# The first two products of down's first groups as split products, their tokens' low parts made in the group ahead

## The chip, the cores and the metric

One core of one Trainium2 chip. The metric is the device time in microseconds (us) of one execution of the whole program. Engines: PE is TensorE, PEld its weight loads, DVE is VectorE, ACT is ScalarE, POOL is GpSimd, SP is the engine that issues most DMAs.

## What is computed

One layer of a hybrid decoder in fp32: an input projection, a short convolution and an mLSTM, an output projection, and then a SwiGLU feed-forward block, which is all that matters here:

```python
hn = _rmsnorm(x, n2g)
x = x + (jax.nn.silu(hn @ wg) * (hn @ wu)) @ wd
```

There are 512 + 64 tokens, `D_MODEL` is 2048 and `D_FF` 5632, which is `FT` = 44 tiles of 128.

## The kernel before, in words

**Split products.** fp32 accuracy is had from the rounded type fp32r. Each operand is split into a high part (a copy rounded to fp32r, made by ACT) and a low part (the operand less its high part, made by DVE). A product is then three matmuls for each tile of 128 rows: high by high, high by low and low by high (L836, L838, L840 in `product`). With `GK` = 8 tiles that is 24 matmuls of 128x128 weights by 288 tokens.

**Groups of seven products.** The feed-forward block is done two by two in blocks with Strassen's scheme in Winograd's form: each group is seven products (p = 0 to 6) instead of eight. Groups 0 to 43 are gate and up; the 16 *down groups* d = 0 to 15 (`FT + d`) are the down product's first 32 tiles of hidden values, in two halves (`NCH` = 2) of `PPC` = 8 groups. The rest of down follows in an ordinary way. Products 0, 2, 4 and 6 of a group accumulate into one PSUM bank, `bank_a`. After product 4 DVE must take a sum out of it (`upper_up`, L2149, in gate and up; `add_block(d, 1)`, L2265, in down), and signals that by `c22_ok`; only then may product 6 go on in the same bank:

```python
pe.wait_ge(c22_ok, g + 1)
product(m, u, 6, bank_a, False)
```

**Order on each engine.** Each engine has one stream of instructions, written out by hand, and waits at semaphores. ACT makes a product's high weights into a ring of three slots (`product_hi`, L1259), when the product three back has been used. DVE makes the low weights (`product_low`, L2095; it counts `g_lo`), and sums of weight blocks (`weight_sum`, L2077 to L2090; n = 1 is for the group to come). DVE runs ahead of PE by some products, so the last sums of group g stand in DVE's code for group g + 1: `down_group(0)` begins on DVE with `upper_up` of group 43, and `down_group(d)` with `add_block(d - 1, 1)`.

**The first group of each half.** The operands on the token side (seven tensors `opraw[j]`, j = 0 to 6) change at d = 0 and d = 8. SP loads `opraw[j]` (L478) when product j of the group ahead has been used. ACT makes the high parts (`hidden_hi`, L1335, two halves of 128x1152) and DVE the low ones (`hidden_low`, L2244, two halves). The low part `oplo[j]` is written over `opraw[j]`, in the same memory. Down groups 0 and 8 use the raw operands: `whole_product` (L851) is 8 plain fp32 matmuls on a whole copy of the weights (`whole_copy`, L1268); on DVE `whole_ready` does only semaphore work. `hidden_low(c, j)` waits until product j of that group has read the raw tokens. ACT makes `hidden_hi` of j = 0 and 1 in the group ahead already (L1324 to L1328 and L1386 to L1392). On DVE `hidden_low` of j = 0 to 3 stands in down group 0 or 8 (L2298 to L2316), of j = 4 to 6 in the group behind it.

Of the kernel before, what the change touches and what calls it, by code (L numbers as in the profile page):

```python
# [60 lines left out]
def hybrid_trunk_step(nc, x_prompt, x_sample, state_conv, state_C, state_n, state_m, norm1_g, w_in,  # L61
# [14 lines left out]
    FT = FF // P  # L76
# [23 lines left out]
    X_PIECES = ((0, 2), (2, 2), (4, 4), (8, 4), (12, 4))  # L100
    SMALLS = 10
    SQ_ACT = 4
    X_LAST = {k0 + n - 1: b for b, (k0, n) in enumerate(X_PIECES)}
    assert sum(n for _, n in X_PIECES) == KT
    QS = float(DK) ** -0.5
    GK = KT // 2
    GU = 6
# [5 lines left out]
    NCH, PPC = FS // KT, KT // 2  # L113
# [7 lines left out]
    with ExitStack() as ctx:  # L121
# [461 lines left out]
        def _(pe):  # L583
# [326 lines left out]
            def down_group(d):  # L910
                g = FT + d
                m, u = g // GU, g % GU
                bank_a, bank_b, bank_c = BANK_A[u % 3], 1, 4
                for p, bank, start, ready, n in ((0, bank_a, True, c21_ok, g - 2), (1, bank_c, True, c12_ok, g),
                                                 (2, bank_a, False, p1c_ok, g + 1), (3, bank_b, True, c11_ok, g),
                                                 (4, bank_a, False, u2c_ok, g + 1), (5, bank_c, False, p5c_ok, g + 1),
                                                 (6, bank_a, False, c22_ok, g + 1)):
                    pe.wait_ge(ready, n)
                    if d % PPC == 0:
                        whole_product(m, u, p, bank, start, d // PPC)  # L920
                    else:
                        if d % PPC == 1:
                            pe.wait_ge(op_lo, 15 + 14 * (d // PPC) + 2 * p + 2)
                        product(m, u, p, bank, start)
                    if p == 3 and d > PPC:
                        turn_pair(d - 1)
# [76 lines left out]
        def _(act):  # L1003
# [354 lines left out]
            def down_group(d):  # L1358
                g = FT + d
                m, u = g // GU, g % GU  # L1360
                c, bank_a, bank_c = d // PPC, BANK_A[u % 3], 4
                starts = d % PPC == 0
                ends = d % PPC == PPC - 1 and c + 1 < NCH
                weights = whole_copy if starts else product_hi
                weights(m, u, 0)
                weights(m, u, 1)
                if d == 0:
                    gate_sigmoid(g)
                weights(m, u, 2)
                if starts:  # L1370
                    hidden_hi(c, 2)
                keep_copy(m, u, 0, p1c, bank_a, c11_ok, p1c_ok)
                weights(m, u, 3)
                if starts:
                    hidden_hi(c, 3)
                weights(m, u, 4)
                keep_copy(m, u, 1, p5c, bank_c, c22_ok, p5c_ok)
                if starts:
                    hidden_hi(c, 4)
                keep_copy(m, u, 2, u2c, bank_a, c12_ok, u2c_ok)  # L1380
                if d == 0:
                    h_store(m, u)
                weights(m, u, 5)
                if starts:
                    hidden_hi(c, 5)
                if ends:  # L1386
                    hidden_hi(c + 1, 0)
                weights(m, u, 6)
                if starts:
                    hidden_hi(c, 6)  # L1390
                if ends:
                    hidden_hi(c + 1, 1)  # L1392
                if 1 <= d <= PPC:
                    sum_store(d - 1)
                elif d > PPC:
                    turned_out(d - 1)
# [146 lines left out]
        def _(dve):  # L1543
# [548 lines left out]
            def product_low(m, u, p):  # L2092
                dve.wait_ge(g_hi, m * (7 * GU) + (7 * u + p + 1))
                slot = (7 * u + p) % 3
                tt(gw_ring[:, slot, 1], source(u, p), gw_ring[:, slot, 0].bitcast(F32), ALU.subtract).then_inc(g_lo, 1)  # L2095
# [90 lines left out]
                             (th4[:, 0, :], b21, th32[:, 1, :]))[n]  # L2186
                tt(out, a, b, ALU.subtract).then_inc(t_step, 1)

            def group(m, u, norm=None):

                g = m * GU + u
                v = (u - 1) % GU
                pair = u % 2 == 0 and (not isinstance(m, int) or g <= FS)

                def sums(n):
                    if pair:
                        pair_sum(m if u else m - 1, v, n)

                upper_up(g - 1, v)
                product_low(m, u, 0)  # L2200
                weight_sum(m, u, 2)
                lower_gate(g - 1)
                if norm:
                    norm[0]()
                else:
                    gate_scaled(g - 1)
                weight_sum(m, u, 3)
                product_low(m, u, 1)
                if norm:
                    norm[1]()  # L2210
                product_low(m, u, 2)
                if norm:
                    dve.wait_ge(r2_ok, 1)
                    gate_scaled(g - 1)
                weight_sum(m, u, 4)
                gate_product(g - 1)
                product_low(m, u, 3)
                gate_rstd(g - 1)
                product_low(m, u, 4)
                hidden(g - 1, v)  # L2220
                sums(0)
                product_low(m, u, 5)
                sums(1)
                upper_gate(g, u)
                sums(2)
                if u < GU - 1:
                    weight_sum(m, u + 1, 1)
                else:
                    weight_sum(m + 1, 0, 1)
                sums(3)  # L2230
                product_low(m, u, 6)

            def whole_ready(m, u, p):

# [3 lines left out]

            def hidden_low(c, j):

                dve.wait_ge(g_used, 7 * (FT + c * PPC) + j + 1)
                for n, (k0, k1) in enumerate(((0, 4), (4, GK))):
                    dve.wait_ge(op_hi, 15 + 14 * c + 2 * j + n + 1)
                    tt(oplo[j][:, k0:k1, :], opraw[j][:, k0:k1, :], ophi[j][:, k0:k1, :].bitcast(F32),  # L2244
                       ALU.subtract).then_inc(op_lo, 1)
# [21 lines left out]
            def down_group(d):  # L2267
# [4 lines left out]
                starts = d % PPC == 0  # L2272
                ends = d % PPC == PPC - 1 and c + 1 < NCH
                second = d % PPC == 1
                low = whole_ready if starts else product_low
                upper_up(g - 1, (u - 1) % GU) if d == 0 else add_block(d - 1, 1)
                low(m, u, 0)
                weight_sum(m, u, 2)
# [16 lines left out]
                gate_rstd(g - 1) if d == 0 else add_block(d - 1, 3)  # L2295
                if second:
                    hidden_low(c, 6)
                if starts:  # L2298
                    hidden_low(c, 0)
                low(m, u, 4)  # L2300
                if d == 0:
                    hidden(g - 1, (u - 1) % GU)
                if starts:
                    hidden_low(c, 1)
                low(m, u, 5)
                if starts:
                    hidden_low(c, 2)
# [7 lines left out]
                if starts:  # L2315
                    hidden_low(c, 3)  # L2316
                else:
                    low(m, u, 6)

            def norm_start():  # L2320
                dve.wait_ge(ss2_mm, 1)
# [22 lines left out]
                for w in range(GU):  # L2344
                    group(m, w)
            for g in range(FS // GU * GU, FT):
                group(g // GU, g % GU)
            for d in range(NCH * PPC):
                down_group(d)

# [147 lines left out]
```

## Time and profile before

| | |
|---|---|
| median of 3 runs | 2502.27 us (2502.08 to 2504.0) |
| profiled execution | 2503.21 us, span 2501.5 us |
| PE busy | 2460.6 us (98%) |
| DVE busy | 1771.9 us (71%) |
| ACT busy | 894.8 us (36%) |
| mean granted clock of TensorE | 0.996 |

Times in the trace are us from the start of the span. A row of a timeline is: start, duration, engine, line, operation, output <- inputs, shapes, number of instructions merged; in brackets the engine's idle time before it and what ended it. PE's matmuls overlap in the records, so their pace is read from starts. A granted clock of 1.00 is 2.4 GHz, of 0.50 the half level, 1.2 GHz.

### The profile page before, as it was taken

What the parts mean: (1) busy time and instruction counts of PE and PEld (TensorE: products, weight loads), DVE (VectorE), ACT (ScalarE), POOL (GpSimd) and SP (SyncE); (2) the same over time, 40 slices, a digit from 0 to 9 for tenths busy, and PEclk for the clock granted to TensorE, in tenths of its full rate; (3) what the DMA queues carried; (4) which work ended last, traced back from release to release, by engine and by line L of the source; (5) the groups of instructions that cost most, each with busy time, mean ns of one, the idle gap of its engine ahead of it and who ended that gap; (6) DMA issues with size and microseconds to landing.
All of it is one profiled execution on the core that took longest, in us unless ns stands there. A gap on an engine that the chain in (4) does not pass through costs nothing.

```text
span 2501.5 us, 44517 instructions
## 1 busy us (share of the span) xinstructions
PE 2460.6 (98%) x17602; PEld 2394.8 (96%) x17602; DVE 1771.9 (71%) x2487; ACT 894.8 (36%) x1236; POOL 37.2 (1%) x60
## 2 busy tenths in 40 slices
PE   8999999999999998999999999999999999999998
PEld 7999999999999997999999999999999999999886
DVE  7576575575687668887787777877777867766435
ACT  5212222222233335343333433434444533544313
POOL 0000000000000000000000000000000000000100
PEclk9999999999999999999999999999999999999999
DMA  5333233333335665343343433443333755744722
GB/s 124 99 117 102 76 117 101 90 104 94 89 113 155 190 194 188 112 127 113 107 126 110 120 116 110 127 118 116 106 108 108 253 150 152 271 132 141 272 82 76
DMA packets 458922, 325.54 MB, mean 130 GB/s; under 512 B 14130, under 2 KB 429006, under 8 KB 456368
## 3 DMA queue, kind: packets, MB, share of 16 engines
q1 hardware_dynamic: 403704, 250.29, 33.9%
q10 hardware_dynamic: 51448, 58.42, 7.6%
q0 software_dynamic: 3584, 14.16, 1.5%
q8 instruction: 140, 2.29, 0.4%
q14 instruction: 46, 0.38, 0.0%
HBM read 264.49 MB, written 58.34 MB: 129 GB/s over the span
## 4 chain that ended last, share of the span: by engine, by line
PE 94%; DVE 3%; DMA 1%; ACT 1%; issue 1%; SPq 0%; DVEq 0%; ACTq 0%
PE ps L603 21%; PE ps L836 17%; PE ps L840 17%; PE ps L838 17%; PE ps L606 11%; PE ps L611 3%; PE ps L851 2%; PE ps L947 2%; PE ps L949 2%; PE ps L951 2%; DVE gw_ring L2095 0%; PE ps L955 0%; DMA xtok<-in_x_sample_dram 0%; PE ps L956 0%; PE ps L863 0%
## 5 line engine op out<-in xcount | busy, mean ns | idle before, releaser
L836 PE MATMUL ps<-ophi,gw_ring 128*128 128x288 f32 x3248 | 963.9, 297 | 15.8 <-ACT p1c L1286 6.6
L838 PE MATMUL ps<-oplo,gw_ring 128*128 128x288 f32 x3248 | 959.6, 295 | 0.0
L840 PE MATMUL ps<-ophi,gw_ring 128*128 128x288 f32 x3248 | 957.9, 295 | 0.0
L836 PEld LDWEIGHTS ps<-ophi,gw_ring 128*128 128x128 f32 x3248 | 610.8, 188 | 18.3 <-ACT p1c L1286 7.0
L840 PEld LDWEIGHTS ps<-ophi,gw_ring 128*128 128x128 f32 x3248 | 613.3, 189 | 0.0
L838 PEld LDWEIGHTS ps<-oplo,gw_ring 128*128 128x128 f32 x3248 | 611.5, 188 | 0.2
L1012 ACT ACTIVATE whi<-wraw 128x512 fp32r<-128x512 f32 x256 | 160.6, 631 | 600.9 <-PE ps L606 449.4
L603 PE MATMUL ps<-xhi,whi 128*128 128x288 f32 x1536 | 333.7, 299 | 0.0
L606 PE MATMUL ps<-xhi,wlo 128*128 128x288 f32 x1536 | 329.5, 296 | 0.0
L603 PE MATMUL ps<-xlo,whi 128*128 128x288 f32 x1536 | 329.4, 296 | 0.0
L2095 DVE TENSOR_TENSOR gw_ring<-graw_a,gw_ring 128x1024 fp32r<-128x1024 f32 x195 | 238.7, 1224 | 116.8 <-ACT gw_ring L1259 116.2
L1259 ACT ACTIVATE gw_ring<-graw_a 128x1024 fp32r<-128x1024 f32 x195 | 206.4, 1059 | 271.3 <-PE ps L840 256.5
L1559 DVE TENSOR_TENSOR wlo<-wraw,whi 128x512 fp32r<-128x512 f32 x256 | 179.3, 700 | 139.6 <-ACT whi L1012 138.0
L603 PEld LDWEIGHTS ps<-xhi,whi 128*128 128x128 f32 x1536 | 248.0, 189 | 4.0 <-issue 3.0
L603 PEld LDWEIGHTS ps<-xlo,whi 128*128 128x128 f32 x1536 | 248.4, 189 | 0.0
L606 PEld LDWEIGHTS ps<-xhi,wlo 128*128 128x128 f32 x1536 | 248.1, 189 | 0.0
L2095 DVE TENSOR_TENSOR gw_ring<-wsum,gw_ring 128x1024 fp32r<-128x1024 f32 x116 | 141.7, 1222 | 83.4 <-ACT gw_ring L1259 83.4
L1554 DVE TENSOR_TENSOR wraw<-wraw,vecs 128x512 f32<-128x512 f32 x224 | 149.0, 683 | 45.0 <-DMA wraw<-in_w_in_dram 20.7
L1259 ACT ACTIVATE gw_ring<-wsum 128x1024 fp32r<-128x1024 f32 x116 | 122.6, 1057 | 116.1 <-PE ps L840 109.7
L2095 DVE TENSOR_TENSOR gw_ring<-graw_b,gw_ring 128x1024 fp32r<-128x1024 f32 x95 | 116.3, 1224 | 54.1 <-ACT gw_ring L1259 53.6
L1259 ACT ACTIVATE gw_ring<-graw_b 128x1024 fp32r<-128x1024 f32 x95 | 100.6, 1059 | 130.5 <-PE ps L840 128.4
L603 PE MATMUL ps<-mixhi,whi 128*128 128x288 f32 x512 | 109.9, 296 | 0.6 <-DVE wlo L1559 0.6
(336 smaller groups left out, 2661.6 us busy)
## 6 DMA issues: line engine op xcount, KB each, us to landing
wraw<-in_w_in_dram SPq DMA_DIRECT2D x96, 512.0 KB, 3.8
graw_a<-in_w_ffn_gate_dram SPq DMA_DIRECT2D x59, 512.0 KB, 3.7
graw_a<-in_w_ffn_up_dram SPq DMA_DIRECT2D x59, 512.0 KB, 4.9
graw_a<-in_w_ffn_down_dram SPq DMA_DIRECT2D x42, 512.0 KB, 5.7
wraw<-in_w_out_dram SPq DMA_DIRECT2D x32, 512.0 KB, 4.1
opraw<-hop SPq DMA_DIRECT2D x14, 1152.0 KB, 10.3
graw_b<-in_w_ffn_gate_dram SPq DMA_DIRECT2D x29, 512.0 KB, 3.7
graw_b<-in_w_ffn_up_dram SPq DMA_DIRECT2D x29, 512.0 KB, 4.6
```

The source lines that it names most:

```text
L603: pe.matmul(out[:, a, :], whi[:, q, s, :], moving[:, 2 * k + a, :], start=first and moving is hi, stop=False)
L606: mm = pe.matmul(out[:, a, :], wlo[:, q, s, :], hi[:, 2 * k + a, :], start=False, stop=last)
L611: one = lambda out, lhsT, rhs, start=True, stop=True: pe.matmul(out, lhsT, rhs, start=start, stop=stop)
L836: pe.matmul(out, gw_ring[:, slot, 0, k, :], ophi[p][:, k, :], start=start and k == 0, stop=False, skip_group_check=True)
L838: pe.matmul(out, gw_ring[:, slot, 0, k, :], oplo[p][:, k, :], start=False, stop=False, skip_group_check=True)
L840: mm = pe.matmul(out, gw_ring[:, slot, 1, k, :], ophi[p][:, k, :], start=False, stop=k == GK - 1, skip_group_check=True)
L851: mm = pe.matmul(ps[:, bank, 0:HT], gw_whole[:, slot, 0, k, :], opraw[p][:, k, :], start=start and k == 0, stop=k == GK - 1, skip_group_ch ...
L1012: act.activation(whi[:, q, 0:n, :], wraw[:, q // 2, s0:s0 + n, :], ACT.Copy).then_inc(hi_done, 1)
L1259: act.activation(gw_ring[:, (7 * u + p) % 3, 0], source(u, p), ACT.Copy).then_inc(g_hi, 1)
L1554: tt(w, w, g, ALU.mult).then_inc(gained, 1)
L1559: tt(wlo[:, q, 0:n, :], wraw[:, q // 2, s0:s0 + n, :], whi[:, q, 0:n, :].bitcast(F32), ALU.subtract).then_inc(lo_done, 1)
L2095: tt(gw_ring[:, slot, 1], source(u, p), gw_ring[:, slot, 0].bitcast(F32), ALU.subtract).then_inc(g_lo, 1)
```

## The change

Products 0 and 1 (`SPLIT_OPS` = 2) of down groups 0 and 8 become split products: PE runs `product` for them and waits for their tokens' low parts (`op_lo`), ACT makes `product_hi` and DVE `product_low` for their weights. `hidden_low` of j = 0 and 1 moves on DVE from down group 0 or 8 into the last group ahead of it: `hidden_low(c, 0)` ahead of that group's `product_low` 6 and `hidden_low(c, 1)` behind it, without the wait for `g_used`. (`ends` is assigned twice; that changes nothing.)

```diff
@@ -100,6 +100,7 @@
     X_PIECES = ((0, 2), (2, 2), (4, 4), (8, 4), (12, 4))
     SMALLS = 10
     SQ_ACT = 4
+    SPLIT_OPS = 2
     X_LAST = {k0 + n - 1: b for b, (k0, n) in enumerate(X_PIECES)}
     assert sum(n for _, n in X_PIECES) == KT
     QS = float(DK) ** -0.5
@@ -916,10 +917,10 @@
                                                  (4, bank_a, False, u2c_ok, g + 1), (5, bank_c, False, p5c_ok, g + 1),
                                                  (6, bank_a, False, c22_ok, g + 1)):
                     pe.wait_ge(ready, n)
-                    if d % PPC == 0:
+                    if d % PPC == 0 and p >= SPLIT_OPS:
                         whole_product(m, u, p, bank, start, d // PPC)
                     else:
-                        if d % PPC == 1:
+                        if d % PPC <= 1:
                             pe.wait_ge(op_lo, 15 + 14 * (d // PPC) + 2 * p + 2)
                         product(m, u, p, bank, start)
                     if p == 3 and d > PPC:
@@ -1361,7 +1362,7 @@
                 c, bank_a, bank_c = d // PPC, BANK_A[u % 3], 4
                 starts = d % PPC == 0
                 ends = d % PPC == PPC - 1 and c + 1 < NCH
-                weights = whole_copy if starts else product_hi
+                weights = lambda m, u, p: (whole_copy if starts and p >= SPLIT_OPS else product_hi)(m, u, p)
                 weights(m, u, 0)
                 weights(m, u, 1)
                 if d == 0:
@@ -2186,7 +2187,7 @@
                              (th4[:, 0, :], b21, th32[:, 1, :]))[n]
                 tt(out, a, b, ALU.subtract).then_inc(t_step, 1)
 
-            def group(m, u, norm=None):
+            def group(m, u, norm=None, last=False):
 
                 g = m * GU + u
                 v = (u - 1) % GU
@@ -2228,7 +2229,11 @@
                 else:
                     weight_sum(m + 1, 0, 1)
                 sums(3)
+                if last:
+                    hidden_low(0, 0)
                 product_low(m, u, 6)
+                if last:
+                    hidden_low(0, 1)
 
             def whole_ready(m, u, p):
 
@@ -2238,7 +2243,8 @@
 
             def hidden_low(c, j):
 
-                dve.wait_ge(g_used, 7 * (FT + c * PPC) + j + 1)
+                if j >= SPLIT_OPS:
+                    dve.wait_ge(g_used, 7 * (FT + c * PPC) + j + 1)
                 for n, (k0, k1) in enumerate(((0, 4), (4, GK))):
                     dve.wait_ge(op_hi, 15 + 14 * c + 2 * j + n + 1)
                     tt(oplo[j][:, k0:k1, :], opraw[j][:, k0:k1, :], ophi[j][:, k0:k1, :].bitcast(F32),
@@ -2272,7 +2278,8 @@
                 starts = d % PPC == 0
                 ends = d % PPC == PPC - 1 and c + 1 < NCH
                 second = d % PPC == 1
-                low = whole_ready if starts else product_low
+                ends = d % PPC == PPC - 1 and c + 1 < NCH
+                low = lambda m, u, p: (whole_ready if starts and p >= SPLIT_OPS else product_low)(m, u, p)
                 upper_up(g - 1, (u - 1) % GU) if d == 0 else add_block(d - 1, 1)
                 low(m, u, 0)
                 weight_sum(m, u, 2)
@@ -2295,13 +2302,9 @@
                 gate_rstd(g - 1) if d == 0 else add_block(d - 1, 3)
                 if second:
                     hidden_low(c, 6)
-                if starts:
-                    hidden_low(c, 0)
                 low(m, u, 4)
                 if d == 0:
                     hidden(g - 1, (u - 1) % GU)
-                if starts:
-                    hidden_low(c, 1)
                 low(m, u, 5)
                 if starts:
                     hidden_low(c, 2)
@@ -2315,7 +2318,11 @@
                 if starts:
                     hidden_low(c, 3)
                 else:
+                    if ends:
+                        hidden_low(c + 1, 0)
                     low(m, u, 6)
+                    if ends:
+                        hidden_low(c + 1, 1)
 
             def norm_start():
                 dve.wait_ge(ss2_mm, 1)
@@ -2344,7 +2351,7 @@
                 for w in range(GU):
                     group(m, w)
             for g in range(FS // GU * GU, FT):
-                group(g // GU, g % GU)
+                group(g // GU, g % GU, last=g == FT - 1)
             for d in range(NCH * PPC):
                 down_group(d)
 
```

## Rows read from the trace of the kernel before

**Rows 1.** The page: the span, and the chain that ended last by engine.

```profile
span 2501.5 us, 44517 instructions
...
PE 94%; DVE 3%; DMA 1%; ACT 1%; issue 1%; SPq 0%; DVEq 0%; ACTq 0%
```

**Rows 2.** The instructions of L851, and ACT's timeline: start us, us, instruction, idle before.

```profile
L851 PE MATMUL ps<-opraw,gw_whole x224: 405/406/406, 1956.6 to 2167.4; 128*128 128x288 f32 x112
...
1976.28 1.06 ACT L1259 ACTIVATE gw_ring<-graw_a 128x1024 fp32r<-128x1024 f32 x1 [0.71 <-PE ps L851]
1980.16 1.06 ACT L1259 ACTIVATE gw_ring<-wsum 128x1024 fp32r<-128x1024 f32 x1 [2.82 <-PE ps L851]
```

**Rows 3.** PE's timeline, group 43 into down group 0, and start of down group 8.

```profile
1953.42 0.30 PE L836 MATMUL ps<-ophi,gw_ring 128*128 128x288 f32 x1
...
1956.62 27.32 PE L851 MATMUL ps<-opraw,gw_whole 128*128 128x288 f32 x112
...
2140.43 27.32 PE L851 MATMUL ps<-opraw,gw_whole 128*128 128x288 f32 x112
```

**Rows 4.** DVE's timeline, groups 43 and down group 0.

```profile
1928.04 0.46 DVE L2149 TENSOR_TENSOR up<-ps,p5c 128x288 f32<-128x288 f32 x1 [0.47 <-PE ps L840]
...
1947.60 1.22 DVE L2077 TENSOR_TENSOR wsum<-graw_a,graw_b 128x1024 f32<-128x1024 f32 x1
1951.47 1.23 DVE L2095 TENSOR_TENSOR gw_ring<-graw_a,gw_ring 128x1024 fp32r<-128x1024 f32 x1 [2.66 <-ACT gw_ring L1259]
1952.62 0.45 DVE L2149 TENSOR_TENSOR up<-ps,p5c 128x288 f32<-128x288 f32 x1
...
1963.54 2.62 DVE L2244 TENSOR_TENSOR oplo<-opraw,ophi 128x1152 fp32r<-128x1152 f32 x2
1966.07 0.45 DVE L2176 TENSOR_TENSOR h<-up,sact 128x288 f32<-128x288 f32 x1
```

**Rows 5.** ACT's timeline, end of group 43.

```profile
1948.27 2.22 ACT L1335 ACTIVATE ophi<-opraw 128x1152 fp32r<-128x1152 f32 x2 [2.89 <-DMA opraw<-hop]
...
1951.35 2.21 ACT L1335 ACTIVATE ophi<-opraw 128x1152 fp32r<-128x1152 f32 x2
```

**Rows 6.** PE's timeline in the stage's first group.

```profile
979.95 0.40 PE L836 MATMUL ps<-ophi,gw_ring 128*128 128x288 f32 x1 [3.16 <-DVE up L2149]
980.19 0.29 PE L838 MATMUL ps<-oplo,gw_ring 128*128 128x288 f32 x1
```

**Rows 7.** DVE's and ACT's timelines, end of down group 7.

```profile
2131.84 1.22 DVE L2077 TENSOR_TENSOR wsum<-graw_b,graw_a 128x1024 f32<-128x1024 f32 x1
...
2134.79 0.45 DVE L2265 TENSOR_TENSOR cacc<-ps,cacc 128x288 f32<-128x288 f32 x1
...
2130.45 2.23 ACT L1335 ACTIVATE ophi<-opraw 128x1152 fp32r<-128x1152 f32 x2 [1.25 <-DMA opraw<-hop]
...
2133.52 2.20 ACT L1335 ACTIVATE ophi<-opraw 128x1152 fp32r<-128x1152 f32 x2
```

**Rows 8.** PE after idle; busy us by window (PE, PEld, DVE, ACT, POOL; PEclk, DMA); `opraw`'s loads.

```profile
959.98 0.58 PE L836 MATMUL ps<-ophi,gw_ring 128*128 128x288 f32 x1 [3.65 <-ACT p1c L1286]
...
993.91 0.40 PE L836 MATMUL ps<-ophi,gw_ring 128*128 128x288 f32 x1 [2.95 <-ACT p1c L1286]
...
2335.09 0.50 PE L947 MATMUL ps<-dwhi,hhi 128*128 128x512 f32 x1 [3.08 <-DVE hs L2361]
...
960.00:966.00 6.00, 6.00 (x27) 5.89 (x28) 6.00 (x7) 6.00 (x8) 0.00 (x0) 0.61 0.65 267
980.00:986.00 6.00, 6.00 (x45) 6.00 (x46) 5.97 (x6) 0.00 (x0) 0.00 (x0) 1.00 0.59 175
994.00:1000.00 6.00, 6.00 (x34) 6.00 (x35) 4.42 (x6) 3.16 (x5) 0.00 (x0) 0.72 0.41 119
2335.00:2341.00 6.00, 5.91 (x26) 4.92 (x27) 4.91 (x5) 0.71 (x1) 0.00 (x0) 1.00 1.04 399
...
DMA to landing us min/median/max: 4.7/10.3/13.7
```

## The prediction

> **What bounds the kernel.** I read the page first: the span, and the chain that ended last. TensorE (PE) carries 94% of that chain [rows 1], so a change pays only if PE works less or waits less, and it costs whatever PE is made to wait. Next comes the one kind of PE work that the change replaces, the plain fp32 matmul of `whole_product`: 224 records for its 112 instructions, two records each [rows 2]. Then PE's own timeline around group 43 (the last of the gate and up stage) and down group 0. PE never waits there: the last product of group 43 starts at 1953.42, the 112 records of down group 0 at 1956.62, and down group 8 starts at 2140.43, also without a gap [rows 3]. So whatever is saved on PE is saved in full, and any wait that is put there costs in full. Last come the timelines of VectorE (DVE) and ScalarE (ACT) in the same stretch, because the change puts DVE work just ahead of an operation for which PE waits [rows 4, 5].
>
> **What is saved on PE.** Products 0 and 1 of down groups 0 and 8 go from 8 fp32 matmuls to 24 split ones. An fp32 product lasts 3.88 us: ACT may overwrite a weight slot when the product that used it is done, and two such releases by L851 lie at 1976.28 and 1980.16 [rows 2]. A split product lasts 3.20 us: product 6 of group 43, 24 matmuls, fills 1953.42 to 1956.62 [rows 3]. That is 0.68 us for each product, and 4 × 0.68 = **2.72 us off PE**. Whether PE passes from split to fp32 matmuls before product 0 or before product 2 is alike: there is one such passage in each of the two groups either way, and the one in rows 3 shows no gap.
>
> **What is added.** On ACT nothing: the copy into the ring takes the place of the copy of whole weights one for one, and `hidden_hi` of tokens 0 and 1 stands in the last group already. On DVE four `product_low` are new, 1.14 us each (from 1951.47 to the next start at 1952.62 [rows 4]), where `whole_ready` did only semaphore work. Their cover is DVE's free time in the group; what they delay is worked out below. The two pairs of `hidden_low` are moved, not added: one pair is two subtractions and holds DVE for 2.53 us (1963.54 to 1966.07 [rows 4]). No transfer is moved on SP or POOL; SP's later loads wait for DVE's or PE's counts and slide by some 3 us at most, ahead of uses which slide too.
>
> **Where the moved work lands, and who waits.** This is the step that decides. `hidden_low(0, 0)` is put ahead of `product_low` 6 of group 43 and `hidden_low(0, 1)` behind it. DVE works in order, and queued behind both is the first operation of `down_group(0)`, `upper_up(43)` at L2149. That addition takes the PSUM bank of products 0, 2 and 4 out; PE waits for it (`c22_ok`, L884) before product 6 of *group 43*, which accumulates into the same bank. Before, it started at 1952.62, was done at 1953.07, and PE needed it at 1953.42: a slack of 0.35 us only.
>
> Now the same stretch with the moved work. ACT's first half of tokens 0 starts at 1948.27 [rows 5] and takes some 1.15 us (half of the pair's 2.22 and what two in a row overlap), so DVE, free since about 1948.74, starts the first half at 1949.45 and is through with the pair at 1951.98. `product_low` 6 follows (its weights were there at 1951.47 already) and leaves DVE at 1953.12. The second pair needs ACT's copies of 1951.35, ready by 1953.56 at the latest, so it isn't held up: it runs 1953.12 to 1955.65. `upper_up(43)` then runs 1955.65 to 1956.10, and PE can start product 6 at 1956.15 instead of 1953.42. **A new wait of 2.73 us.** To this I add the slow restart: at 979.95, after exactly this wait for `upper_up`, the second matmul came 0.24 us after the first [rows 6] instead of 0.13 (3.20 / 24); so 0.11 more, 2.84 in all. Rows 6 are also the proof that the wait exists: there DVE was late with the first group's operand splits, and PE stood 3.16 us.
>
> Group 7 of down does the same. `add_block(7, 1)` signals the same semaphore, and PE's product 6 of down group 7 waits for it. DVE's sum for the next group starts at 2131.84 and holds it 1.13 us, to 2132.97; ACT's copies have been made (2130.45 and 2133.52, two halves each, 2.2 us) by the time each is wanted [rows 7]. First pair 2132.97 to 2135.50, `product_low` 6 to 2136.64, second pair to 2139.17, `add_block` done at 2139.62, PE from 2139.67. Before, it ran at 2134.79, and product 6 started at 2140.43 − 3.20 = 2137.23 [rows 3, 7]. **A new wait of 2.44 us,** 2.55 with the restart.
>
> Are the new `product_low` late next? In down group 0 that of product 0 ends at 1957.25, and PE wants it at 1956.15 + 3.20 + 0.11 = 1959.46. Then come a weight sum (1.14), `lower_gate` and `gate_scaled` (1.1 together, allowing for their hand-over), a weight sum (1.14), and `product_low` 1 ends at about 1961.90; PE wants it at 1962.66. So no further wait, with 0.8 us to spare; in down group 8 it is about 2144.6 against 2146.2. ACT's copy of product 0's result, for which product 2 waits, comes out near 1964.4 against 1965.9. These margins exist only because product 6 has been late already: were it on time, `product_low` 0 and 1 of down group 0 would be late themselves, by 0.6 and then another 0.6 us or so.
>
> **The sum.** −2.72 + 2.84 + 2.55 = +2.67 us. The profiled execution took 2503.21 us for a span of 2501.5; this makes 2505.9 of it. It lay 0.9 over the median of the three runs, 2502.27, and against that the forecast is **2504.9 us**, slower by 0.11%. The bounds: the restart between 0 and 0.11 each, DVE's hand-overs another 0.1 to 0.3 each way, and some 1 us for how executions scatter: 2503.4 to 2506.4 for this case alone. About 0.2%, 5.0 us, is what a measurement of this kernel can tell from no change.
>
> **Rivals.** First, *the wait doesn't bite*, chance 0.08. In steady groups `upper_up` has a long lead: at 1928.04 [rows 4], for a product 6 that begins seven products before 1953.42, at 1931.02. If DVE had such a lead here only the saving would be left: 2502.27 − 2.72 = 2499.6 us. Against it: DVE can't start before ACT has the tokens, and 5.06 us of subtractions don't fit in a slack of 0.35.
>
> Second, the one on the slow side: *the new waits make TensorE's clock fall*, chance 0.12. PE stood idle 3.65 us before 959.98, 3.16 before 979.95, 2.95 before 993.91 and 3.08 before 2335.09 [rows 6, 8]. Around the first and third the granted clock fell to the half level, 1.2 GHz: its mean is 0.61 over 960 to 966 and 0.72 over 994 to 1000. Behind the second and fourth it stayed at 1.00. What sets the two pairs apart the rows don't say. A fall costs 6 × 0.39 = 2.3 or 6 × 0.28 = 1.7 us. Here PE would stand about 2.57 and 2.27 us by its records (0.16 less than the delays, since the last matmul's record runs on), less than in any of the four, with 20 us and more of dense matmuls before. One fall makes 2506.6 to 2507.2; both make 2.67 + 3.4 to 4.6, so 2508.3 to 2509.5, and this is where slower by over 0.2% decides. The Trainium skill ("TensorE: Matmul & The Clock Gate", "HAM oscillation") says that a wait between dense matmuls can send the array back to its half clock, and that the moment varies from run to run; that speaks against this change, and the trace agrees in two gaps of four.
>
> Third, *tokens 0 land late*, chance 0.06. ACT waited for tokens 0 before the change too [rows 5], and a token load takes 10.3 us in the median and 13.7 at worst [rows 8]. With 3.4 us more in group 43, DVE's chain and so `upper_up` come 3.4 us later: 2508.3 us. Nothing ahead of these loads is changed, so only scatter speaks for it.
>
> **How the numbers follow.** The forecast has 0.74. The range leaves out the first rival, both falls of the clock and the late landing: 2501.5 to 2507.8. Faster by over 0.2% (below 2497.3) is reached by no case, 0.02. Slower by over 0.2% (above 2507.3): 0.07 for two falls, 0.04 for late tokens, 0.01 beside, so 0.12. Within 0.2%: 0.86.
>
> **What the profile after would show.** The L851 records down from 224 to 160, those of L836 up by 32. PE idle at L836 before the last product of group 43 and of down group 7, put down to L2149 and L2265, near 2.6 and 2.3 us. DVE's L2149 of group 43 near 1955.7, behind two L2244, one L2095 and two more L2244. No PE idle before products 0 and 1 of down groups 0 and 8. The granted clock 1.00 behind both gaps. I am wrong if PE shows no gap there (then 2499.6), if the gap moves to `product_low` at L2095, or if the clock falls.

## The result, and the profile after

| | before | after |
|---|---|---|
| median of 21 runs each | 2502.66 us (2501.66 to 2505.52) | 2507.24 us (2504.83 to 2510.43) |
| ratio of after to before | | 1.0019, 95% interval 1.0013 to 1.0025 |
| profiled execution | 2503.21 us, span 2501.5 | 2508.91 us, span 2507.1 |
| mean granted clock | 0.996 | 0.993 |

The change makes the kernel slower by 0.19%, 3.3 to 6.3 us by the interval. I had forecast 2504.9, slower by 0.11%; the measured median lies inside my range of 2501.5 to 2507.8, near its upper end, and beyond what I gave to the likeliest case (up to 2506.4).

The page after (span, chain by engine) and the row of the fp32 matmuls, as before in [rows 1, 2]:

```profile
span 2507.1 us, 44577 instructions
...
PE 93%; DVE 3%; DMA 1%; issue 1%; ACT 1%; SPq 0%; DVEq 0%; ACTq 0%
...
L852 PE MATMUL ps<-opraw,gw_whole x160: 405/406/406, 1967.2 to 2171.3; 128*128 128x288 f32 x160
```

The records of the fp32 matmul are down from 224 to 160, the four products of 16 records each. Lines below the edit are moved by one to six: L837, L839 and L841 are the split matmuls, L852 the fp32 one, L2150 `upper_up`, L2271 `add_block`, L2250 `hidden_low`.

PE's timeline after, to be held against [rows 3]:

```profile
1956.00 0.40 PE L837 MATMUL ps<-ophi,gw_ring 128*128 128x288 f32 x1 [2.59 <-DVE up L2150]
1956.24 0.30 PE L839 MATMUL ps<-oplo,gw_ring 128*128 128x288 f32 x1
...
1986.38 0.51 PE L837 MATMUL ps<-ophi,gw_ring 128*128 128x288 f32 x1
...
2142.49 0.40 PE L837 MATMUL ps<-ophi,gw_ring 128*128 128x288 f32 x1 [2.30 <-DVE cacc L2271]
...
2171.36 0.51 PE L837 MATMUL ps<-ophi,gw_ring 128*128 128x288 f32 x1
```

Where PE went from group 43 into down group 0 without a gap, it now stands 2.59 us before product 6 of group 43 (1956.00) and 2.30 us before that of down group 7 (2142.49), each time for the sum out of its own bank. After the restart the second matmul comes 0.24 us behind the first, as in [rows 6]. There is no wait before products 0 and 1 of down groups 0 and 8: the list of PE's waits has, from 1900 on, these two and two in the last stage (3.08 and 0.8 us) that were there before.

DVE's timeline after, for both places, against [rows 4, 7]:

```profile
1947.05 0.46 DVE L2142 TENSOR_TENSOR gz<-ps,p1c 128x288 f32<-128x288 f32 x1 [0.59 <-PE ps L841]
1947.42 1.22 DVE L2078 TENSOR_TENSOR wsum<-graw_a,graw_b 128x1024 f32<-128x1024 f32 x1
1949.28 2.63 DVE L2250 TENSOR_TENSOR oplo<-opraw,ophi 128x1152 fp32r<-128x1152 f32 x2 [0.64 <-ACT ophi L1336]
1951.82 1.22 DVE L2096 TENSOR_TENSOR gw_ring<-graw_a,gw_ring 128x1024 fp32r<-128x1024 f32 x1
1952.95 2.62 DVE L2250 TENSOR_TENSOR oplo<-opraw,ophi 128x1152 fp32r<-128x1152 f32 x2
1955.49 0.45 DVE L2150 TENSOR_TENSOR up<-ps,p5c 128x288 f32<-128x288 f32 x1
...
2134.28 0.45 DVE L2271 TENSOR_TENSOR cacc<-ps,cacc 128x288 f32<-128x288 f32 x1
2134.64 1.22 DVE L2078 TENSOR_TENSOR wsum<-graw_b,graw_a 128x1024 f32<-128x1024 f32 x1
2135.78 2.62 DVE L2250 TENSOR_TENSOR oplo<-opraw,ophi 128x1152 fp32r<-128x1152 f32 x2
2138.31 1.22 DVE L2096 TENSOR_TENSOR gw_ring<-graw_a,gw_ring 128x1024 fp32r<-128x1024 f32 x1
2139.45 2.62 DVE L2250 TENSOR_TENSOR oplo<-opraw,ophi 128x1152 fp32r<-128x1152 f32 x2
2141.99 0.45 DVE L2271 TENSOR_TENSOR cacc<-ps,cacc 128x288 f32<-128x288 f32 x1
```

The order is what the prediction worked out, with its times hit to 0.2 us (this execution reached the stretch 0.17 us earlier than the one of before): the first pair waits for ACT's copy until 1949.28 (I had 1949.45), `product_low` 6 at 1951.82 (1951.98), the second pair at 1952.95 (1953.12), and `upper_up` at 1955.49 (1955.65). In down group 7 the same run takes 2134.64 to 2141.99.

What I did not forecast stands in the granted clock. Three windows of after (busy us of PE, PEld, DVE, ACT and POOL with their instructions, then PEclk, DMA share and GB/s), one behind each new wait and one at the start of the last stage:

```profile
1952.00:1960.00 8.00, 5.41 (x30) 5.18 (x29) 7.90 (x9) 3.77 (x5) 0.00 (x0) 0.81 1.02 429
2140.00:2148.00 8.00, 5.70 (x43) 5.51 (x42) 7.73 (x9) 2.82 (x3) 0.00 (x0) 1.00 1.01 425
2334.00:2346.00 12.00, 8.92 (x38) 7.30 (x38) 9.11 (x9) 4.67 (x5) 0.00 (x0) 0.86 1.03 370
```

The clock fell behind the first new wait and not behind the second. The pace of the matmuls shows the same. Two starts in that stretch, 0.24 us apart where it is 0.13 at full clock:

```profile
1957.13 0.44 PE L839 MATMUL ps<-oplo,gw_ring 128*128 128x288 f32 x1
1957.37 0.44 PE L841 MATMUL ps<-ophi,gw_ring 128*128 128x288 f32 x1
```

It fell at the start of the last stage too (0.86), where the profile of before kept it:

```profile
2330.00:2342.00 12.00, 8.92 (x46) 7.51 (x45) 9.27 (x9) 4.84 (x5) 0.00 (x0) 1.00 1.04 371
```

**How the 5.6 us between the two spans come about.** I cut the trace at four points which every kernel here has. *Stretch A* runs from `upper_gate` of group 43 (the sum into `gz` from `p1c`, at 1947.05 above and 1947.22 before) to the first split matmul behind down group 0, the record of 0.51 us (1986.38; before 1983.57). *Stretch B* runs from `add_block(7, 0)` (2134.28; before 2131.47) to the same record behind down group 8 (2171.36; before 2167.38). *Between* is what lies between them.

| | A | between | B | behind B |
|---|---|---|---|---|
| before | 36.35 | 147.90 | 35.91 | 334.12 |
| after | 39.33 | 147.90 | 37.08 | 335.74 |
| difference | +2.98 | 0.00 | +1.17 | +1.62 |

B is my sum to 0.02 us: 2.55 − 1.36 = +1.19. A is +1.48 by my sum, and 1.5 us more for the clock. In the last column the clock fell at the start of the last stage, a place that the change doesn't touch, and the run up to A was 0.17 us shorter.

The expectations below that give A and B as 36.82 and 36.38 for the kernel before end both stretches at a release on ACT, 0.47 us later than the table does. The differences can be compared all the same. Those that speak of 36.35 and 35.91 end them as the table does.

### The profile page after: what moved, and what is told of

It reads as the page before. It is cut to its first block, busy times and chain, and to the rows that moved or that the text cites. A ratio compares the mean times of both kernels' runs of the same rounds, so it can differ in the third digit from the quotient of the medians.

```text
span 2507.1 us, 44577 instructions
## 1 busy us (share of the span) xinstructions
PE 2463.6 (98%) x17634; PEld 2400.5 (96%) x17634; DVE 1776.6 (71%) x2491; ACT 894.7 (36%) x1236; POOL 36.8 (1%) x60
## 4 chain that ended last, share of the span: by engine, by line
PE 93%; DVE 3%; DMA 1%; issue 1%; ACT 1%; SPq 0%; DVEq 0%; ACTq 0%
PE ps L604 21%; PE ps L837 17%; PE ps L841 16%; PE ps L839 16%; PE ps L607 11%; PE ps L612 3%; PE ps L948 2%; PE ps L950 2%; PE ps L952 2%; PE ps L852 2%; DVE gw_ring L2096 0%; DMA opraw<-hop 0%; PE ps L956 0%; PE ps L957 0%; DMA xtok<-in_x_sample_dram 0%
## 5 line engine op out<-in xcount | busy, mean ns | idle before, releaser
L837 PE MATMUL ps<-ophi,gw_ring 128*128 128x288 f32 x3280 | 975.0, 297 | 18.0 <-DVE up L2150 6.1
L839 PE MATMUL ps<-oplo,gw_ring 128*128 128x288 f32 x3280 | 970.6, 296 | 0.0
L841 PE MATMUL ps<-ophi,gw_ring 128*128 128x288 f32 x3280 | 968.6, 295 | 0.0
L837 PEld LDWEIGHTS ps<-ophi,gw_ring 128*128 128x128 f32 x3280 | 618.1, 188 | 20.5 <-DVE up L2150 6.5
L841 PEld LDWEIGHTS ps<-ophi,gw_ring 128*128 128x128 f32 x3280 | 620.7, 189 | 0.0
L839 PEld LDWEIGHTS ps<-oplo,gw_ring 128*128 128x128 f32 x3280 | 619.0, 189 | 0.2
```

What stands on the lines that cost most here:

```text
L837: pe.matmul(out, gw_ring[:, slot, 0, k, :], ophi[p][:, k, :], start=start and k == 0, stop=False, skip_group_check=True)
L839: pe.matmul(out, gw_ring[:, slot, 0, k, :], oplo[p][:, k, :], start=False, stop=False, skip_group_check=True)
L841: mm = pe.matmul(out, gw_ring[:, slot, 1, k, :], ophi[p][:, k, :], start=False, stop=k == GK - 1, skip_group_check=True)
```

## The experiments

Two theories had to be told apart. *W*: these groups cost or save what PE works and what PE waits for DVE, with a fall of the clock behind some waits. *S*: the split products themselves, or the transfers beside them, cost the 1.9 us by which the change is worse than my sum (4.58 between the medians, less 2.67). The forecast's own weak step, the chance of a fall, had to be measured as well. With a scatter of several us between executions, the stretches of the profiles tell more than the ratios of the medians of whole executions; both are given.

**1. The products without the moved work.** The changed kernel, leaving out the low parts of tokens 0 and 1 in all down groups: PE uses the high part in their place, for the same number of matmuls, and `hidden_low` of these only signals. DVE's part of the edit:

```diff
                     dve.wait_ge(op_hi, 15 + 14 * c + 2 * j + n + 1)
+                    if j < SPLIT_OPS:
+                        dve.sem_inc(op_lo, 1)
+                        continue
```

> The change without its four pairs of hidden_low: this kernel leaves out the low parts of tokens 0 and 1 in all sixteen down groups (PE uses the high part in their place, same number of matmuls) and DVE only signals. Theory W (the waits for upper_up and add_block are what costs; split products save 2.72 us): PE idle before product 6 of group 43 and of down group 7 is gone, upper_up of group 43 is back near 1952.6, one small wait of about 0.6 us before product 1 of down group 0 (its product_low comes 1 us late because ACT's copy does), sum -2.72 + 0.7 = -2.0 us against the kernel before, ratio 0.9992. Rival S (the 1.9 us that the change costs beyond my sum come from the split products or from the transfers beside them): this kernel is at +0.0 to -0.2 us, ratio 1.0000.

Measured: ratio 1.0004, interval 0.9995 to 1.0013. The two ends of B in this run's timelines of DVE and PE:

```profile
2128.69 0.45 DVE L2274 TENSOR_TENSOR cacc<-ps,cacc 128x288 f32<-128x288 f32 x1
...
2163.24 0.51 PE L837 MATMUL ps<-ophi,gw_ring 128*128 128x288 f32 x1
```

A is 35.39 and B 34.55 us, between them 148.22: −0.96, −1.36 and +0.32 against before, together −2.00 us as theory W has it. B has no PE wait at all, so −1.36 is the bare price of two products: 0.68 us each, exactly the step of the prediction. PE waits 0.15 us in A, in the list of its waits. The whole execution missed this expectation: its interval, −1.3 to +3.3 us, doesn't hold the −2.0 us of theory W (0.9992) and does hold S (1.0000). The kernel before, run beside it 27 times, ranged from 2497.54 to 2508.39. The profile shows where the gain went: behind B it has 335.66 us, 1.54 more than before, with a fall of the clock at the start of the last stage, and with that the sum is −0.46 us, inside the interval. So S, which puts the extra into the products or their transfers, is refuted for A, between and B, and only for them; experiment 7 comes back to what lies behind.

**2 and 3. The waits without the products.** The kernel before, with its products and its order; ahead of the last `product_low` of group 43 and of down group 7 DVE repeats that subtraction, whole or in part (`again` is (8, 8, 3) in group 43 and (8, 8, 8, 4) in down group 7, and empty elsewhere; the numbers are how many of the 8 tiles are repeated):

```diff
+                for k in again:
+                    link(tt(gw_ring[:, slot, 1, 0:k], source(u, p)[:, 0:k], gw_ring[:, slot, 0, 0:k].bitcast(F32), ALU.subtract))
                 tt(gw_ring[:, slot, 1], source(u, p), gw_ring[:, slot, 0].bitcast(F32), ALU.subtract).then_inc(g_lo, 1)
```

> The kernel before, all products as they were, with repeated low-part subtractions ahead of the last product_low of group 43 (3.0 us) and of down group 7 (4.4 us), so that upper_up and add_block come as late as in the changed kernel. Theory W with the clock: PE idle 2.6 and 2.3 us in those two places, together +5.4 us by themselves; if the clock falls behind such a gap as it did in the profile of the changed kernel, 1.5 to 2 us more for each fall, so +7.2 us or so on average (ratio 1.0029). Rival S: the gaps cost +5.4 us and the clock stays, ratio 1.0022. If PE does not wait for these two additions at all: +0.0, ratio 1.0000.

Measured: 2510.39 us, ratio 1.0038, interval 1.0024 to 1.0051. PE's timeline at the two places and the clock behind each:

```profile
1954.61 0.40 PE L836 MATMUL ps<-ophi,gw_ring 128*128 128x288 f32 x1 [2.18 <-DVE up L2151]
...
2142.73 0.40 PE L836 MATMUL ps<-ophi,gw_ring 128*128 128x288 f32 x1 [2.55 <-DVE cacc L2267]
...
1952.00:1960.00 8.00, 5.82 (x31) 5.48 (x30) 5.88 (x8) 2.82 (x4) 0.00 (x0) 0.79 1.02 429
2140.00:2148.00 8.00, 5.45 (x28) 5.20 (x27) 5.24 (x7) 1.25 (x2) 0.00 (x0) 0.79 1.02 427
```

So PE waits in the kernel before as soon as `upper_up` and `add_block` come late, with nothing of the change in it. A is 40.30 and B 40.23: +3.95 and +4.32. Of that 2.18 and 2.55 are idle, 0.16 each the overlap of the last record and 0.11 the restart; 1.5 us of each is left, and the clock fell behind both (0.79).

> The waits alone again, same question: idle 2.2 and 2.55 us, a fall behind each with a chance of a half; A 36.82 + 2.45 = 39.3 without and 40.8 with one, B 36.38 + 2.8 = 39.2 or 40.7.

The same kernel profiled once more, one execution (2510.81 us):

```profile
1955.65 0.40 PE L836 MATMUL ps<-ophi,gw_ring 128*128 128x288 f32 x1 [1.94 <-DVE up L2151]
...
2142.87 0.61 PE L836 MATMUL ps<-ophi,gw_ring 128*128 128x288 f32 x1 [3.15 <-DVE cacc L2267]
...
1952.00:1960.00 8.00, 6.06 (x42) 5.61 (x42) 6.89 (x9) 4.34 (x5) 0.00 (x0) 1.00 1.01 423
2140.00:2148.00 8.00, 5.13 (x26) 5.07 (x27) 5.38 (x7) 0.97 (x2) 0.00 (x0) 0.79 1.00 417
```

Here 1.94 us idle left the clock at 1.00, and A is 38.54, +2.19 = 1.94 + 0.27. Behind 3.15 us it fell: B is 40.79, +4.88.

**4. Shorter waits.** The same, with (8, 2) and (8, 8, 4) repeats.

> The kernel before with fewer repeated subtractions than in the run of the waits alone: PE idle about 1.0 us in group 43 and 1.3 us in down group 7 instead of 2.2 and 2.55. Theory C (a wait of 2.2 us and more lets the clock fall, a short one seldom): clock 1.00 behind both, stretch A 36.82 + 1.2 = 38.0, B 36.38 + 1.6 = 38.0. Rival (any wait here lets it fall): 1.5 us more in each, 39.5.

```profile
1953.43 0.40 PE L836 MATMUL ps<-ophi,gw_ring 128*128 128x288 f32 x1 [0.72 <-DVE up L2151]
...
2138.80 0.40 PE L836 MATMUL ps<-ophi,gw_ring 128*128 128x288 f32 x1 [1.30 <-DVE cacc L2267]
...
1952.00:1960.00 8.00, 7.28 (x44) 6.36 (x43) 6.48 (x8) 5.73 (x7) 0.00 (x0) 1.00 1.01 424
2140.00:2148.00 8.00, 8.00 (x42) 6.74 (x42) 2.94 (x4) 4.99 (x6) 0.00 (x0) 1.00 1.02 429
```

A 37.32 (+0.97) and B 37.46 (+1.55): the idle time and the restart, no fall. That is theory C for short waits; what it says of waits of 2.2 us and more fails in experiment 5.

**5 and 6. The change twice more**, one execution each (2506.38 and 2506.84 us), unedited.

> The changed kernel once more, for a second look at its two waits. Theory: idle again 2.6 and 2.3 us, A = 36.82 + 1.48 = 38.3 where the clock stays and 39.8 where it falls, B = 36.38 + 1.19 = 37.6 or 39.1. So far the clock fell behind three of four such waits (one of two in the changed kernel, both in the run of the waits alone); at least one fall is expected here. If the fall in the first look was a chance of one in eight, as my prediction had it, none.

```profile
1955.14 0.40 PE L837 MATMUL ps<-ophi,gw_ring 128*128 128x288 f32 x1 [2.20 <-DVE up L2150]
...
2140.11 0.40 PE L837 MATMUL ps<-ophi,gw_ring 128*128 128x288 f32 x1 [2.29 <-DVE cacc L2271]
...
1952.00:1960.00 8.00, 5.80 (x44) 5.56 (x43) 7.90 (x10) 3.33 (x5) 0.00 (x0) 1.00 1.01 423
2140.00:2148.00 8.00, 7.89 (x59) 7.89 (x60) 6.19 (x7) 4.14 (x5) 0.00 (x0) 1.00 1.02 428
```

The expectation of a fall was missed: none here. A is 37.44, B 37.08, and behind B 335.5.

> The changed kernel a third time: idle 2.2 to 2.6 and 2.3 us; so far the clock fell behind 3 of 6 waits of 2.2 to 2.6 us (1 of 2, 2 of 2, 0 of 2) and behind none of the waits under 1.7. If each falls with a chance of a half, one fall is the likeliest; if the first looks were luck and the chance is one in eight, none.

Its two windows, and PE's wait in group 43; the wait in down group 7 was 2.29 us again:

```profile
1953.98 0.40 PE L837 MATMUL ps<-ophi,gw_ring 128*128 128x288 f32 x1 [2.69 <-DVE up L2150]
...
1952.00:1960.00 8.00, 6.02 (x34) 6.02 (x35) 7.59 (x9) 2.86 (x4) 0.00 (x0) 0.79 1.00 419
2140.00:2148.00 8.00, 7.53 (x56) 7.53 (x57) 6.54 (x8) 3.79 (x5) 0.00 (x0) 1.00 1.02 430
```

One fall, behind the longer wait: A 39.44, B 37.08, and behind B 335.7. Between this profile and the one above, A differs by 2.00 us, of which 0.49 is idle time (2.69 against 2.20). So **a fall costs 1.5 us**.

**7. The kernel before once more.**

> The kernel before once more: A 36.8 and B 36.4 again, with no PE idle in either. At the start of the last stage, where PE waits 3.1 us for the first hidden values, the clock fell in all five later profiles and not in the one of before: if that is chance it falls here too, and this profile is 1.5 to 3 us longer than the first in that place.

2502.02 us; A 36.34, between 147.91, B 35.91: the stretches repeat to 0.01 us. At the start of the last stage the clock stayed again, against the expectation. It stayed in the second run of the waits alone too (behind B 334.1 us in all three), and fell in the other ten profiles (335 to 337). PE's wait there is 3.08 us in all thirteen. The kernel with the waits alone has one profile with the fall and one without, so the split products aren't needed for it, nor does it come each time. That the change makes it likelier isn't ruled out: it fell in ten of eleven profiles of edited kernels, all three of the change among them, and in neither of the two of before.

**8. The second pair behind the sum.** The changed kernel with `hidden_low` of token 1 moved from the end of the last group into the next one, behind `upper_up` or `add_block`:

```diff
-                if last:
-                    hidden_low(0, 1)
...
                 upper_up(g - 1, (u - 1) % GU) if d == 0 else add_block(d - 1, 1)
+                if starts:
+                    hidden_low(c, 1)
                 low(m, u, 0)
```

> The changed kernel with hidden_low of token 1 moved behind upper_up / add_block and ahead of product_low 0 of the next group. Theory W: PE's wait before product 6 shrinks from 2.6 to 0.2 us in group 43 and from 2.3 to 0 in down group 7; in exchange product_low 0 and 1 of the next group are late: waits at L2095's successor of about 0.4 and 1.4 us in down group 0, 0.4 and 0.5 in down group 8. Together 2.1 us less than my sum for the change, so +0.6 us against the kernel before, and no fall of the clock since no gap is over 1.5 us: ratio 1.0002. Rival S: the extra 1.9 us stay, +2.5 us, ratio 1.0010.

Measured: ratio 1.0006, interval 0.9997 to 1.0016. PE's timeline in stretch A:

```profile
1958.05 0.37 PE L837 MATMUL ps<-ophi,gw_ring 128*128 128x288 f32 x1 [0.30 <-DVE gw_ring L2096]
...
1962.69 0.37 PE L837 MATMUL ps<-ophi,gw_ring 128*128 128x288 f32 x1 [1.21 <-DVEq L2240]
```

The wait before product 6 is gone from PE's list of waits, and the waits for `product_low` 0 and 1 are there in the size expected (0.30 and 1.21, in down group 8 0.31 and 0.35). The second is put down to DVE's sequencer, L2240 being `whole_ready`; it is the wait for `product_low` 1, which comes just ahead of it on DVE. A 37.25, between 148.31, B 35.65: +1.05 us, where I had +0.6 and the change itself has +2.3 without a fall. *Between* has 0.41 us more, part of it a wait of 0.17 us for `product_low` in down group 1, and behind B the profile has 336.8 us. The ratio's interval holds the rival's 1.0010 too; the stretches tell the two apart.

**9 to 11. The split products with the order mended.** DVE stood idle ahead of the first pair and later in the group. First order: `hidden_low` of token 0 ahead of the last `product_low`, of token 1 in halves around `product_low` 0, then `product_low` 1, and the weight sums only after that; on ACT, the copies of products 0 and 2 ahead of `hidden_hi` 2 and 4:

```diff
                 upper_up(g - 1, (u - 1) % GU) if d == 0 else add_block(d - 1, 1)
+                if starts:
+                    hidden_low(c, 1, (0,))
                 low(m, u, 0)
+                if starts:
+                    hidden_low(c, 1, (1,))
+                    lower_gate(g - 1) if d == 0 else add_block(d - 1, 2)
+                    low(m, u, 1)
                 weight_sum(m, u, 2)
```

> Split products kept, order mended: hidden_low of token 0 ahead of the last product_low (in DVE's idle time there), token 1's first half behind upper_up / add_block, its second half behind product_low 0, then the bank sum for product 1, product_low 1, and only then the weight sums; on ACT the copies of products 0 and 2 go ahead of hidden_hi 2 and 4. Theory W: only the wait before product 6 of group 43 is left, 0.2 us and 0.1 of restart; -2.72 + 0.3 = -2.4 us against the kernel before, ratio 0.9990. Rival S: -0.5 us, ratio 0.9998. If DVE or ACT become late somewhere else, PE shows a wait in down group 0 or 8 at that place.

Measured: ratio 1.0012, interval 1.0002 to 1.0023. Missed, by a wait that no kernel had before:

```profile
1980.93 4.15 PE L852 MATMUL ps<-opraw,gw_whole 128*128 128x288 f32 x16 [1.62 <-DVE cacc L2275]
```

PE waited 1.62 us before product 6 of *down group 0*, for `add_block(0, 1)` behind `hidden_low` 3, and 1.39 in down group 8. A, between and B are +0.51, +0.84 and +0.29 us against before. It is the same mistake as the change's, one group on. So this sum was taken ahead of `hidden_low` 3:

> The reordered kernel, with add_block(d, 1) of down groups 0 and 8 taken ahead of hidden_low of token 3, because its profile showed PE waiting 1.6 and 1.4 us for that sum before product 6 of those groups. Stretch A (from upper_gate of group 43 to ACT's last release by an fp32 product of down group 0) was 36.82 us before the change, 39.81 after, 37.34 reordered; stretch B (from add_block(7, 0) to the last such release in down group 8) 36.38, 37.56, 36.67. Theory W (all that these groups cost or save is PE's work and its waits for DVE): A 35.5 to 35.6, B 35.0 to 35.1, no PE idle over 0.3 us in either, together -2.6 us against before; median ratio 0.9990, with an interval that may hold 1 since the clock's falls elsewhere scatter by more. Rival: another operation of DVE or ACT is late in its place, A or B above 36.

Measured: ratio 1.0012, interval 1.0003 to 1.0022. A and B came as expected (35.06 and 34.56, −1.29 and −1.35), and the rest did not. PE's timeline in down group 1:

```profile
1995.54 0.37 PE L837 MATMUL ps<-ophi,gw_ring 128*128 128x288 f32 x1 [1.39 <-DVE gw_ring L2101]
...
1999.57 0.37 PE L837 MATMUL ps<-ophi,gw_ring 128*128 128x288 f32 x1 [0.60 <-DVE gw_ring L2101]
```

With PE earlier, DVE was late in the group behind, and *between* grew from 147.90 to 150.94; the three sum to +0.40 us. Behind B the profile has 337.3 us, 3.2 more than before, with a wait of 1.38 us for `product_low` in down group 9 and the clock's fall at the start of the last stage. Last, `hidden_low` of tokens 2, 3 and 4 each one place earlier, into the idle time of down groups 0 and 8, and `add_block(d, 1)` ahead of the weight sum too:

```diff
-                if second:
-                    hidden_low(c, 4)
                 low(m, u, 2)
...
                 if d == 0:
                     hidden(g - 1, (u - 1) % GU)
+                if starts:
+                    hidden_low(c, 2)
                 low(m, u, 5)
                 if starts:
-                    hidden_low(c, 2)
+                    hidden_low(c, 3)
...
                 if starts:
                     low(m, u, 6)
+                    add_block(d, 1)
...
                 if starts:
-                    add_block(d, 1)
-                    hidden_low(c, 3)
+                    hidden_low(c, 4)
```

> The run before had stretches A and B as expected (35.06 and 34.56 us to the first split matmul behind the group, against 36.35 and 35.91 before) but gave 3.0 us back in down group 1 and 1.4 in down group 9, where DVE was late with product_low. Here hidden_low of tokens 2, 3 and 4 each come one place earlier, into DVE's idle time in down groups 0 and 8 (2.4 and 2.8 us while it waited for ACT's copies). Theory W: A 35.1, B 34.6, and the stretch between them back at 147.9 us; -2.64 us against before, ratio 0.9990 with an interval that may hold 1. Rival: DVE is simply full there, and the wait moves again: the stretch between A and B stays over 148.5.

Measured: 2501.33 us against 2503.67, ratio 0.9991, interval 0.9982 to 1.0.

```profile
1943.00 0.46 DVE L2147 TENSOR_TENSOR gz<-ps,p1c 128x288 f32<-128x288 f32 x1 [0.58 <-PE ps L841]
...
1977.97 0.51 PE L837 MATMUL ps<-ophi,gw_ring 128*128 128x288 f32 x1
...
1991.39 0.37 PE L837 MATMUL ps<-ophi,gw_ring 128*128 128x288 f32 x1 [0.23 <-DVE gw_ring L2101]
...
2160.93 0.51 PE L837 MATMUL ps<-ophi,gw_ring 128*128 128x288 f32 x1
```

A is 34.97 and B 34.55 (it begins at 2126.38 in this run): the whole saving of 2.72 us and no wait in either. One wait of 0.23 us is left in down group 1, and *between* is 148.41. The three sum to −2.23 us, the size of the measured difference of the medians (−2.34). But this profile too has the fall at the start of the last stage, 335.7 us behind B, and with it the sum is −0.65 us; so the agreement of the three stretches with the median isn't a proof. The interval of the ratio just reaches 1: likely faster, and not shown beyond noise.

## Why the prediction was right or wrong

| step | forecast | measured |
|---|---|---|
| saving of an fp32 product made split | 0.68 us | 0.68 (B of experiment 1: −1.36 for two) |
| wait before product 6 of group 43 | 2.57 idle | 2.59, 2.20, 2.69 in three profiles |
| wait before product 6 of down group 7 | 2.27 idle | 2.30, 2.29, 2.29 |
| slow restart | 0.11 us each | 0.11 |
| waits for `product_low` 0 and 1 | none | none |
| stretches A and B, a fall taken off | +1.48, +1.19 | +1.48, +1.09, +1.59; +1.17 each time |
| falls of the clock | 0.12 in all, 1.7 to 2.3 us each | 2 behind 6 waits, 1.5 us each |

**Right**: what bounds the kernel, the saving, the step that decides (DVE's in-order queue puts 5.06 us of subtractions ahead of the sum that PE needs next), its size, and that nothing else comes late. In A the wait varies with the landing of tokens 0, for which ACT waits; in down group 7, where DVE has work until the copies are there, it is the same in all three profiles. My third rival, a landing 3.4 us late, wasn't seen.

**Wrong**: the second rival's chance, and through it the middle of the forecast. I gave 0.12 to a fall, because the new waits were shorter than the four in the profile of before (2.95 to 3.65 us), two of which had one. In the ten waits of 1.9 to 3.2 us that the runs made in these two places, the clock fell behind five: behind all four of 2.55 us and more (2.55, 2.59, 2.69, 3.15), behind one of the other six (2.18, but not 1.94, 2.20, 2.29, 2.29, 2.30). It fell behind none of the shorter waits from A to just behind B, up to 1.62 us. The changed kernel alone had 2 in 6, that is 0.7 falls or 1.0 us per execution. The three profiles of the change have A, between and B together at +4.15, +2.25 and +4.25 us, mean +3.55; the interval of the ratio is +3.3 to +6.3, and 2.67 lies outside it. The sum needed a term of chance times price for each wait, and I had made it a rival of low chance instead. With that term it is 2.67 + 1.0 = +3.7 us, still 0.9 short of the 4.58 between the medians. My case of one fall (2506.6 to 2507.2) has nearly the measured median of 2507.24, but partly by luck: it took a fall at 1.7 to 2.3 us where it cost 1.5, and it counted none of what lies behind B. The range held by 0.6 us, with a time that its likeliest case (up to 2506.4) didn't have.

**Open**: why the clock stays behind one wait of 2.2 us and falls behind another. Open too is the 0.9 us that is left. The three profiles of the change have 1.62, 1.40 and 1.54 us more behind B than before, by the fall at the start of the last stage, which neither profile of before has. If that were so in every execution, the sum would be +5.1 us, also within +3.3 to +6.3; if it is chance (the clock fell there in 10 of all 13 profiles), the rest is scatter in this and in the falls near 30, 960 and 990, whose number differs from execution to execution. No run tells the two apart.

The rule of the Trainium skill ("TensorE: Matmul & The Clock Gate", "HAM oscillation — how this bites in real kernels") that waits between dense matmuls can send the array back to its half clock spoke against the change. Its example has waits of about 3 to 5 us; the traces agree in five of the ten waits here, of which nine were shorter than 3 us.

## What to carry to other kernels

In a kernel that one engine bounds, work moved "earlier" on a helper engine is moved ahead of something: find the next operation in that queue for which the bound engine waits, and its slack. Here it was 0.35 us, and 5.06 us were put before it, for a saving of 2.72. Filling the helper's idle time on both sides of that operation kept 2.23 us of the saving in the stretches that were changed, but only after two further operations had been mended: the sum at the end of the same group, and then the low parts of the group behind, where the bound engine came earlier and used up the slack. And a wait of two microseconds on TensorE had a price beyond its length, the clock's fall, by chance: put it into the sum.

## What the runs showed of the hardware

- Waits shorter than any behind which the clock had fallen in the profile of before had a fall behind them: in the two places the shortest was 2.18 us. Behind waits of 2.55 us and more it fell every time in these two places, and yet it stayed behind 3.08 us at the start of the last stage, in both profiles of before [rows 8] and in the second run of the waits alone, and fell there behind the same 3.08 us in the other ten.
- Elsewhere the clock fell behind still shorter ones, and the 1.5 us of experiment 8's expectation is no safe bound: it fell behind 1.74 us in that run, 1.53 us (at 241.93) in the profile of the change and 1.40 us in that of experiment 10. Each of these times PE waited for nothing that the profile shows. These three are few of the 25 waits of 1.4 to 1.8 us in the thirteen profiles. PE's timeline and the window behind, of experiment 8 and then 10:

```profile
1236.16 0.39 PE L837 MATMUL ps<-ophi,gw_ring 128*128 128x288 f32 x1 [1.74 <-issue]
...
1236.00:1244.00 8.00, 7.84 (x47) 7.84 (x48) 4.08 (x5) 1.36 (x2) 0.00 (x0) 0.79 0.24 68
...
418.09 0.53 PE L612 MATMUL ps<-rows_hi,sel 128*128 128x512 f32 x2 [1.40 <-issue]
...
418.00:426.00 8.00, 7.91 (x44) 7.59 (x45) 1.54 (x4) 2.67 (x7) 1.15 (x3) 0.79 0.25 70
```

- A fall costs 1.5 us here. At the half clock a 128x128 by 128x288 fp32r matmul starts every 0.24 us, at full clock every 0.133, so it is less than twice as slow.
- The stretches of one kernel repeat to 0.01 us between executions (A, between and B of the two profiles of before; between and B of the two of the change without a fall in them) as long as the clock doesn't fall in them and PE's waits are the same; the rest of the scatter between profiles of one kernel lies ahead of A and behind B: the two of before reach A at 1947.22 and 1945.85 us, the three of the change at 1947.05, 1946.57 and 1944.93.
